# The up projection of a hybrid decoder's ConvFFN in fp32 pairs: 2x2 block products, the token stage in three passes

## What is computed

```python
hp = hp + concat(rmsnorm(o_sb, gn_sb), rmsnorm(o_mlp, gn_mlp)) @ w_out        # 1024 -> 1024
gate, up = split(rmsnorm(hp, norm_ffn_g) @ w_up)                              # 1024 -> 2 x 2816
conv = conv_b + sum_j conv_w[j] * shifted(gate, j)                            # causal, width 3, prefix zero or state
hp = hp + (gelu(conv) * up) @ w_down                                          # 2816 -> 1024
hp = hp + sigmoid(rmsnorm(hp, norm_ple_g) @ w_ple_gate) * (p_i @ w_ple_proj)  # 1024 -> 1024, 256 -> 1024
y  = rmsnorm(hp, final_norm_g)
```

## Time and profile before

| | us |
|---|---|
| median of 3 runs | 3101.62 (3099.98 to 3101.78) |
| span of the profiled execution | 3100.2 |
| token stage in it, first to last product | 1145 to 3095 |
| PE busy | 3043.5 (98%) |
| VectorE busy | 2028.5 (65%) |
| ScalarE busy | 1638.4 (53%) |
| GpSimd busy | 147.4 (5%) |

### The profile page before, as it was taken

One profiled execution on the slowest core, in us unless ns is written; L12 is line 12 of the kernel. 1 busy time (PEld: TensorE's weight loads), 2 busy tenths in 40 slices (PEclk: granted clock), 3 DMA queues, 4 the chain that ended last, 5 costly groups with the idle time before them and its releaser, 6 DMA issues.

```text
span 3100.2 us, 51907 instructions
## 1 busy us (share of the span) xinstructions
PE 3043.5 (98%) x18572; PEld 2806.6 (91%) x18572; DVE 2028.5 (65%) x2725; ACT 1638.4 (53%) x2359; POOL 147.4 (5%) x277
## 2 busy tenths in 40 slices
PE   8999999899999999999999999999999999999998
PEld 6888888677778779999999999999999999999998
DVE  4222443779977987764777647776477764778745
ACT  5444311899999975543445434454354543545433
POOL 0000000222222200000000000000000000000000
PEclk9999999999999999999999999999999999999999
DMA  5324456766666655433544335443354433534332
GB/s 184 98 95 138 116 154 165 200 165 178 189 164 168 178 142 153 119 112 111 159 141 120 112 111 160 140 121 111 111 160 140 121 111 111 161 117 118 114 111 76
DMA packets 609905, 422.85 MB, mean 136 GB/s; under 512 B 40857, under 2 KB 566082, under 8 KB 609698
## 3 DMA queue, kind: packets, MB, share of 16 engines
q1 hardware_dynamic: 568676, 318.24, 36.1%
q0 software_dynamic: 20544, 67.19, 7.5%
q10 hardware_dynamic: 20512, 35.17, 3.2%
HBM read 367.26 MB, written 53.25 MB: 136 GB/s over the span
## 4 chain that ended last, share of the span: by engine, by line
PE 63%; DVE 0%; issue 0%; DVEq 0%; ACT 0%; ACTq 0%
PE pf_acc L60 21%; PE pf_acc L58 21%; PE pf_acc L59 20%; PE pf_ps_t L1710 1%; PE pf_ps_sum L1649 0%; PE pf_ps_sum L1658 0%; PE pf_ps_sum L1663 0%; PE pf_ps_t L1720 0%; PE pf_ps_t L1781 0%; DVE late_c L2056 0%; DVE late_ssum L1988 0%; DVEq L1586 0%; DVE late_u L1978 0%; DVE pf_h L2182 0%; ACT late_sq L1809 0%
## 5 line engine op out<-in xcount | busy, mean ns | idle before, releaser
L1802 ACT ACTIVATE late_w_hi<-ahead_raw 128x1024 fp32r<-128x1024 f32 x439 | 463.7, 1057 | 540.4 <-PE pf_acc L60 539.2
L60 PE MATMUL pf_acc<-pf_x_hi,late_w_lo 128*128 128x416 f32 x2080 | 734.1, 353 | 0.0
L58 PE MATMUL pf_acc<-pf_x_hi,late_w_hi 128*128 128x416 f32 x2080 | 733.1, 352 | 0.0
L59 PE MATMUL pf_acc<-pf_x_lo,late_w_hi 128*128 128x416 f32 x2080 | 726.0, 349 | 0.0
L1972 DVE TENSOR_TENSOR late_w_lo<-ahead_raw,late_w_hi 128x1024 fp32r<-128x1024 f32 x439 | 536.0, 1221 | 271.1 <-ACT late_w_hi L1802 270.3
L58 PE MATMUL pf_acc<-late_f_hi,late_w_hi 128*128 128x416 f32 x1280 | 453.3, 354 | 4.0 <-DVEq L2195 4.0
L60 PE MATMUL pf_acc<-late_f_hi,late_w_lo 128*128 128x416 f32 x1280 | 452.2, 353 | 0.0
L59 PE MATMUL pf_acc<-late_f_lo,late_w_hi 128*128 128x416 f32 x1280 | 447.6, 350 | 0.0
L59 PEld LDWEIGHTS pf_acc<-pf_x_lo,late_w_hi 128*128 128x128 f32 x2080 | 390.8, 188 | 8.0 <-issue 1.6
L58 PEld LDWEIGHTS pf_acc<-pf_x_hi,late_w_hi 128*128 128x128 f32 x2080 | 390.4, 188 | 3.7 <-issue 1.6
L60 PEld LDWEIGHTS pf_acc<-pf_x_hi,late_w_lo 128*128 128x128 f32 x2080 | 390.0, 187 | 2.3
(11 more groups left out here) (238 smaller groups left out, 4056.7 us busy)
## 6 DMA issues: line engine op xcount, KB each, us to landing
ahead_raw<-in_w_up_dram SPq DMA_DIRECT2D x220, 512.0 KB, 3.9
ahead_raw<-in_w_down_dram SPq DMA_DIRECT2D x80, 512.0 KB, 4.1
high_pages<-in_cache_k_dram POOLq DMA_DIRECT2D x128, 256.0 KB, 4.1
ahead_raw<-in_w_out_dram SPq DMA_DIRECT2D x40, 512.0 KB, 5.3
ahead_raw<-in_w_ple_gate_dram SPq DMA_DIRECT2D x40, 512.0 KB, 4.0
high_pages<-in_cache_v_dram POOLq DMA_DIRECT2D x64, 256.0 KB, 3.7
at_kT<-in_cache_v_dram POOLq DMA_DIRECT2D x64, 256.0 KB, 5.0
ahead_raw<-in_w_down_dram SPq DMA_DIRECT2D x40, 384.0 KB, 3.5
```

Source lines behind the costliest of these rows:

```text
L58: nc.tensor.matmul(out, stat_hi, mov_hi, start=first, stop=False)
L59: nc.tensor.matmul(out, stat_hi, mov_lo, start=False, stop=False)
L60: return nc.tensor.matmul(out, stat_lo, mov_hi, start=False, stop=last)
L1802: nc.scalar.activation(w_hi[k % 4][:, :], raw[k % 4][:, :], ACT.Copy).then_inc(hi_split, 1)
```

## The change

The loop over blocks is no longer outermost. The stage becomes three passes over all tokens:

1. Out pass: five blocks of 416. For each the out products, the residual (stored as `H`), and the ffn norm, now applied in full (gain on ScalarE, inverse root on GpSimd) and stored as `XN`.
2. Up pass: three token sets of 696 columns (they overlap by 4), each in two halves of TH = 348. For a column tile j of gate and up (66 groups: 3 sets x 22), the weights are seen as four blocks A11, A12 (gate; upper and lower 512 rows), A21, A22 (up), and the tokens as B11, B12, B21, B22 (512 rows x 348 tokens). Seven products P1 to P7 of such blocks, of 4 row tiles x 3 matmuls each, replace the eight. The sums of weight blocks and the differences of token blocks are made on GpSimd, the merges of products on ScalarE (copies out of PSUM) and VectorE; some products add to a bank that already holds another. The next sets' operands T1 to T4 are built on GpSimd, cast and split between the products. The gated tile goes to memory (`F`).
3. Down pass: five blocks of 416. `F` is loaded back, cast and split; then down, gate and projection as before. The final norm's transposes are laid over the down products of the next block.

All DMAs but the stores of y are issued from SP. All loops are written out. SBUF places are given by hand (`place`), and many tiles share them over time, for instance `up0` and T3's low part with the x rows of the last block. The core of the diff:

```diff
+    NS, TH, NG = 3, 348, 66
+    PRODUCTS = ("P1", "P5", "P2", "P4", "P6", "P3", "P7")
+    OPERANDS = ("B11", "T1", "B21", "T4", "T2", "B22", "T3")
+    sequence = []
+    for g in range(NG):
+        sequence.append((g, "P1"))
+        if g > 1:
+            sequence.append((g - 1, "P7"))
+        sequence += [(g, p) for p in ("P5", "P2", "P4")]
+        if g == 1:
+            sequence.append((0, "P7"))
+        sequence += [(g, "P6"), (g, "P3")]
+    sequence.append((NG - 1, "P7"))
...
             @program_block.sync
...
+                for b in range(NB):
                     for mt in range(8):
+                        n = 8 * b + mt + 7
+                        if n < SLABS_OUT:
+                            load_slab(n)
+                        if mt == 0 and b:
+                            store_h(b - 1)
+                            if b + 1 < NB:
+                                load_mix(b + 1)
...
+                        if mt == 3 and b:
+                            store_xn(b - 1)
+                            if b + 1 < NB:
+                                load_x(b + 1)
...
+                        if mt == 5 and b == 2:
+                            load_staged(0)
+                store_h(NB - 1)
+                load_pair(2)
+                store_xn(NB - 1)
+                for g in range(NG):
+                    if g:
+                        if g + 2 < NG:
+                            load_pair(g + 2)
...
+                        store_f(g - 1)
...
+                store_f(NG - 1)
+                load_f(0, 2)
+                load_f(0, 3)
...
             @program_block.gpsimd
-                nc.gpsimd.memset(carry[:, :, :], 0.0).then_inc(carry_zero, 1)
+                def operands(s):
+                    pool.wait_ge(staged_in, 64 * (s + 1))
+                    nc.gpsimd.tensor_tensor(t("T1"), t("B12"), t("B11"), ALU.subtract).then_inc(t_made, 1)
+                    pool.wait_ge(t_made, 4 * s + 1)
+                    nc.gpsimd.tensor_tensor(t("T2"), t("B22"), t("T1"), ALU.subtract).then_inc(t_made, 1)
+                    nc.gpsimd.tensor_tensor(t("T3"), t("B22"), t("B12"), ALU.subtract).then_inc(t_made, 1)
+                    pool.wait_ge(t_made, 4 * s + 2)
+                    nc.gpsimd.tensor_tensor(t("T4"), t("B21"), t("T2"), ALU.subtract).then_inc(t_made, 1)
+                def sums12(g):
...
+                        pool.wait_ge(multiplied, after[g - 2, "P6"])
+                    nc.gpsimd.tensor_tensor(quarter(s12[e], 0), a21, a22, ALU.add).then_inc(s_made, 1)
+                    pool.wait_ge(s_made, 4 * g + 1)
+                    nc.gpsimd.tensor_tensor(quarter(s12[e], 1), quarter(s12[e], 0), a11, ALU.subtract).then_inc(s_made, 1)
+                def sums43(g):
...
+                        pool.wait_ge(multiplied, after[g - 2, "P7"])
+                    nc.gpsimd.tensor_tensor(quarter(s43[e], 1), a11, a21, ALU.subtract).then_inc(s_made, 1)
+                    pool.wait_ge(s_made, 4 * g + 2)
+                    nc.gpsimd.tensor_tensor(quarter(s43[e], 0), a12, quarter(s12[e], 1), ALU.subtract).then_inc(s_made, 1)
...
             @program_block.tensor
+                def multiply(g, p):
+                    e, at_first = g % 2, g % NJ == 0
+                    if at_first:
+                        pe.wait_ge(op_low, 7 * (g // NJ) + PRODUCTS.index(p) + 1)
+                    if p == "P1":
+                        pe.wait_ge(w_low, 4 * g + 1)
...
+                    if p == "P6":
+                        pe.wait_ge(s1_kept, g + 1)
+                        bank = bank_a[e]
+                    if p == "P3":
+                        pe.wait_ge(w_low, 4 * g + 4)
+                        pe.wait_ge(s5_kept, g + 1)
+                        bank = bank_c[e]
+                    if p == "P7":
+                        pe.wait_ge(s2_kept, g + 1)
+                        bank = bank_a[e]
...
             @program_block.scalar
+                for g in range(NG + 1):
+                    if g:
+                        first_tap(g - 1)
...
+                    if g < NG:
+                        keep_s1(g)
...
+                    if g + 1 < NG:
+                        cast_a12(g + 1)
+                    if g:
+                        keep_s3(g - 1)
...
+                    if g < NG:
+                        keep_s5(g)
...
+                    if g + 1 < NG:
+                        cast_s12(g + 1)
...
+                    if g:
+                        gelu(g - 1)
...
+                    if g + 1 < NG:
+                        cast_a22(g + 1)
...
+                        cast_s43(g + 1)
...
+                    if g < NG:
+                        keep_s2(g)
...
             @program_block.vector
+                def low_part(g, n, out, of, hi):
+                    dve.wait_ge(w_cast, 4 * g + n)
+                    dve.wait_ge(s_made, 4 * g + 4)
+                    nc.vector.tensor_tensor(out, of, f32(hi), ALU.subtract).then_inc(w_low, 1)
+                for g in range(NG + 1):
+                    if g:
+                        merge_c12(g - 1)
+                        taps(g - 1)
...
+                    if g == 1:
+                        op_lower(0, 6)
+                    if g:
+                        merge_up(g - 1)
...
+                    if g + 1 < NG:
+                        low_a12(g + 1)
+                        low_s12(g + 1)
...
+                    if g:
+                        gated(g - 1)
+                    if g < NG:
+                        merge_c11(g)
...
+                    if g + 1 < NG:
+                        low_a22(g + 1)
+                        low_s43(g + 1)
```

More of the change, by code:

```diff
@@ L1693, in out_products @@
-                def out_products(b, behind):
-                    q4, u0 = b * (SLABS // 4), b * UNITS
-                    for mt in range(0 if behind else 4, 8):
-                        take(q4, O_AT + mt, u0 + OU + mt + 1)
-                        product(q4, O_AT + mt, OU + mt, f_hi[:, MIX_AT:MIX_AT + 8, :], f_lo[:, MIX_AT:MIX_AT + 8, :], MIX_ORDER,
-                                (mix_lo, 8 * b) if mt == 0 else None, TURNS_OUT.get(mt, {}) if behind else {}, b - 1)
-                        if mt == 0 and behind:
-                            token_mean_square(b - 1)
@@ L1721, in turn_rows, with take @@
                     done.then_inc(rows_turned, 1)
-                def other_products(b, last):
-                    q4, u0 = b * (SLABS // 4), b * UNITS
-                    def up_pair(q4, u, first=False):
-                        for n in range(4):
-                            take(q4, U_AT + n, u + UU + n + 1)
-                            product(q4, U_AT + n, UU + n, x_hi, x_lo, ready=(xlo_done, 16 * b) if first and n == 0 else None)
-                            if first and n == 0:
-                                mean_square(21 * b + 7)
-                    up_pair(q4, u0, True)
-                    with pe.Fori(1, NJ // 2) as jj:
-                        up_pair(q4 + jj, u0 + 4 * jj)
+                def take(n, unit):
+                    pe.wait_ge(low_made, n + 1)
+                    if unit is not None:
+                        if unit >= 4:
+                            pe.wait_ge(acc_free, unit - 3)
+                        else:
+                            pe.wait_ge((s3_kept, c11_made, c12_made, c21_made)[unit], NG - 1)
@@ L1790, in _ @@
+                for g, p in sequence:
+                    multiply(g, p)
+                    if (g, p) == (0, "P5"):
+                        mean_square_out(NB - 1)
+                for b in range(NB):
+                    down(b)
+                    ple(b)
                 token_mean_square(NB - 1)
@@ L1937, in other_acts @@
+                            square(b, 1, 2 * q + e, h_ready, 8 * b + 2 * q + e + 1)
+                        if not last and q < 3:
+                            f_high(b + 1, 3 * q + 2)
                         if q == 3:
-                            high(q4, P_AT + 3 * q + 6, last)
-                for n in range(4):
-                    act.sem_inc(y_stored[n], 16)
-                act.sem_inc(hi_split, 1)
-                act.sem_inc(mix_hi, 4)
-                act.sem_inc(mix_sq, 4)
-                act.sem_inc(mix_rms, 1)
@@ L2242, in program @@
[L2242 to L2251 removed]
+        join = {"raw_loaded": [j.sem(f"raw_loaded{n}") for n in range(4)], "mix_loaded": j.sem("mix_loaded"),
+                "oT_stored": [j.sem(f"oT_stored{s}") for s in range(2)], "stores": 32 * 16 + 32}
@@ L2252, in program @@
+        join["wo_lo"] = [place(nc, f"wo_lo{n}", 39808 + 1024 * n, [P, 1024], F32R) for n in range(4)]
+        join["rs_sb"] = place(nc, "rs_sb", 44736, [P, 416])
+        join["squares"] = [place(nc, f"square{n}", 46880 + BANK * n, [P, BANK]) for n in range(4)]
         with ExitStack() as early:
```

1429 lines of the change are left out of this document (941 added, 488 removed).

## The result

The kernel after takes 3130.1 us (median of 4; 3125.7 to 3131.0) against 3101.4 for the kernel before beside it: ratio 1.009, 95% interval 1.0076 to 1.0105. It is slower by 0.9%; forecast were 3032 us and "faster" at 0.88. The profiled execution has a span of 3128.6 us, 28.4 more than the span before (3100.2).

The account below looks back on a forecast made before the run. TensorE's matmul issue was taken as the bound. Terms of -107 (up projection), +12, +3, +13 (handovers), +5 (out pass) and +4 (gate part) sum to -70 us, from 3101.6 to a forecast of 3032, range 3006 to 3082.

Parts of the forecast that it names:

- The interval: Up projection: 348-column matmuls would issue every 160.4 us/1000 (160.4 ns) instead of 188.7 ns at 416 columns, saving 107.0 us.
- rival (d): Up projection: matmul interval stays at the weight load's 188.7 ns, so the kernel takes 3189 us; chance 0.03.
- The steady group: Up projection: each group takes 13.47 us on TensorE, and the work of the other engines fits within it.
- From up to down, with the four gate parts: Handover from up projection to down, 13 us of idle and slow clock, plus 4 us in the gate and projection part.
- the out pass at 5 us: Out projection: DMA just saturated for blocks 1 to 3, weight lead covers some 20 us of lag; costs 5 us (0 to 40).
- between sets 3 us: Up projection, two changes of token set: operands ready before their products, GpSimd's differences delay one pair of sums; 3 us (0 to 15).
- The handover at 12 us: Out projection to up projection: TensorE idle 10 us (5 to 18), with the slow clock after it 12 us.
- the clock: TensorE at handovers: a 4.0 us idle is followed by 3.4 us at clock 0.50, losing 1.7 us of work.
- (b): Out pass: transfers come late because DMA sustains less than the needed rate; kernel at 3062 us, chance 0.11.
- (c): Up projection groups: GpSimd's sums hold VectorE for their whole length, making its 14.8 us loop the bound; 3121 us, chance 0.06.
- half of (c): Up projection groups: GpSimd's sums hold VectorE 6.0 us, or take 3 us each; 3060 to 3090 us, chance 0.08.

## Why the prediction was wrong

**Right.** The interval: 158.7 ns against 160.4, and rival (d), the load's 188.7, is out. The steady group: 13.4 us against 13.47, and the four sums in it cost nothing (shown by leaving them out). Which waits come last at the start of the up pass and at the down product, and that P7(0) waits for the normalisation of the last block: predicted 7 us, measured 11.7. From up to down, with the four gate parts: 17 predicted, 10 measured by the table.

**Wrong, first step: the out pass at 5 us (+69).** I asked whether the DMA engines could carry 303 GB/s on average, found them "just saturated", and gave the lag to 20 us of lead in the weight slabs. The pass moved 203 GB/s at a share of 0.65, so bandwidth was not the bound in the mean. What failed is that I checked the lead of the weights alone. The mix tiles had none: asked for at row tile 0, behind the store of H, needed behind row tile 3, 14 us after the issue (1199.1 to 1213.3), with 13 us from issue to landing and 10 us of squares, additions, and another block's root and reciprocal behind it. All of these numbers but the landing under load and the additions' length beside GpSimd (3.3 us for three) were in my hands: durations in the earlier trace rows, and 10.0 us for a load of this size in the earlier trace rows, which I used only for the store of XN.

**Second step: "between sets 3 us" (+29).** I had the differences at 3.2 us each (they took 3.2 to 4.2) and wrote that they "delay one pair of sums". Four in a row are 15 us, longer than a group, and nothing else that GpSimd feeds has so much lead. The set changes went wrong otherwise: I counted operand splits at their own length, each "ready 1 to 6 us before its product". VectorE ran at 11.0 us a group (124.25 of 150 us) and not at my 9.1, through the sums (8.9 without them, 99.58 of 150), and its room was gone.

**Third step: the handover at 12 us.** It cost 22 us in groups 0 and 1 and 7.2 before P1(0). I priced the products of the last block at 1 us (the shortest took 1.07); beside VectorE's splits they took 1.78. And I didn't see that the first weights' sums need the place of XN of block 3, nor the squares queued behind them.

**A term that I charged once: the clock.** I took 3.4 us at half clock after one idle of 4.0 us, and charged it twice, 5 us in all. The new waits are many, and nearly each of the long ones is followed by a stretch at a granted clock of 0.5 (1.2 of 2.4 GHz): the 3 us behind the waits of 9.0, 7.9, 14.9, 7.2 (ahead of block 4) and 11.7 us are all at 0.50. In the first window row TensorE is busy for 205.2 us with 999 matmuls that take 188.5 at 188.7 ns: 17 us are the clock's; in the fourth 900.1 against 880: about 20 us. By the 1.7 us of the earlier trace rows a wait of 9 us costs about 11.

**The rivals.** (b), transfers late in the out pass, named the right place with the wrong mechanism and a price of 30 us for 74. (c), the sums that hold VectorE, was the right mechanism in the wrong place: I asked whether it bounds the steady group, where the answer is no, and not what it does to the stretches in which VectorE has no room, where it cost the 13 us of the set changes and a part of the other 14 (the kernel without sums). My price for half of it, "6.0 us of hold", was also wrong in itself: four sums of 1.2 us can hold for 4.8 at most, and half of the 89 us is a hold of about 4.1. The Trainium skill (SBUF — State Buffer, SBUF: two separate sides) says that a GpSimd operation and a VectorE one with two SBUF inputs exclude each other for the whole instruction; the trace agrees: four scalings took 12.35 us beside four differences and 2.34 without them, and the merge with a PSUM input kept its 0.51 us. I had let the rule change only a chance, and not the durations in the sum.

**The range** was 3006 to 3082 and ended inside half of (c), which I had at 3060 to 3090. The upper bounds of the terms together (40, 20, 15, 21 and 15 us) make 3105; I took less, as if the misses were independent. They weren't, as I read it now: the misses come from the same omission, lead times at places where stages meet. And the out pass went past even its own bound, 74 us for 40.

## What to carry to other kernels

When a change takes work from the bounding engine, price the steady state in one line and spend the rest on the places where stages meet: for each load and each serial chain, write down when it is asked for, how long it takes in the queue it stands in, and when it is needed. A load that was early enough at 98% TensorE may be the critical path once the stages are reordered. Treat GpSimd work with SBUF operands as work on VectorE's clock too: put single instructions in idle places of both queues, never several in a row, and add the hold to VectorE's account before asking whether it still fits. A wait's named releaser is the last in a chain; moving that one instruction forward (the set change) gained nothing.

## What the runs showed of the hardware

- GpSimd's two-input sum of 512 fp32 elements takes 1.26 to 1.30 us alone, 1.66 in the mean of the 66 first sums of a group, and over 2 at times; 1392 elements take 3.2 alone.
- A held instruction can wait through several of the other engine's: the split of 1.6 us that took 8.13 began at 1388.77 and ended at 1396.8, while GpSimd ran a difference, a running sum, a second difference and a weight sum with no gap between them. Beside the four differences ahead of block 4, VectorE got in once per difference. What decides between the two no run here tells.
- 348-column matmuls with a weight load each go out every 158.7 ns, 13.7 ns over 348 columns at 2.4 GHz (145.0); at 416 columns it was 15.4 over. The part that doesn't go with the columns is nearly the same.
- DMA in the out pass is bursty: the page's DMA view of the out pass (1145 to 1406 us; busy tenths in 40 slices) is below, and its mean of 0.65 hid landing times of 13 us for one load of 1.7 MB and 8.8 for a weight slab of 0.5 MB, which takes 3.9 in the up projection of the earlier trace rows and 5.3 (median) for the same out weights in the kernel before.

```profile
DMA  8999612479620799894227999990256923950580
```
